# Attention scores with keys on partitions, their maximum and sum by GpSimd; reciprocals and the convolution's SiLU by ScalarE

## The chip, the core and the metric

The kernel runs on one core of a Trainium2 chip. The metric is the device time of one execution in microseconds. TensorE (PE in the profile) multiplies matrices into PSUM, VectorE (DVE) and ScalarE (ACT) work elementwise, GpSimd (POOL) too, and SyncE (SP) issues DMA transfers between HBM and SBUF. All run in parallel, each in its own order, and are tied by semaphores.

## What is computed

One layer: RMSNorm, one input projection, attention over a window and a short gated convolution beside it, one output projection, residual, RMSNorm. The part that the change touches:

```
def swa_sink_attention(q, k, v, sinks, rel_bias):       # 16 chunks of 64 frames, 16 heads, 2 kv heads of 64
    logits = jnp.einsum('bnqkgd,bnskd->bnkgqs', q, kb)   # a chunk's 64 queries x the 128 keys of its band
    logits = logits * (1.0 / math.sqrt(HEAD_DIM)) + band_bias(rel_bias)[None, None]
    logits = jnp.where(valid[...], logits, NEG)
    m = jnp.maximum(jnp.max(logits, axis=-1, keepdims=True), sink)
    p = jnp.exp(logits - m)
    denom = jnp.sum(p, axis=-1, keepdims=True) + jnp.exp(sink - m)
    o = jnp.einsum('bnkgqs,bnskd->bnqkgd', (p / denom), vb)
def short_gated_conv(h, c_gate, b_gate, conv_w, conv_b): # b_gate * causal_conv3(c_gate * h)
...
        mixed = jnp.concatenate([attn * jax.nn.silu(g_attn),
                                 conv * jax.nn.silu(g_conv)], axis=-1)
        x = x + jnp.einsum('bse,ed->bsd', mixed, w_out[l])
```

## The kernel before

**Products.** The two projections are cut into eight blocks (BLOCKS; GATES, QKV, four CONV blocks, OUT0, OUT1), each of 28 steps (LEN): seven partial products p of four steps q. A step multiplies two slices of K for four (QKV: five) tiles of 128x512, and each product is done in three parts with operands split into a high and a low half (product, L1996 to L2011), so a step is 24 matmuls of 512 columns. The high half of the weights is made by ScalarE (w_hi, L970), the low half by VectorE (w_lo, L1344), into a ring of three steps (w_ring); both are issued two steps ahead. The tiles of a finished product leave PSUM through ScalarE (copy_out, L1094) or VectorE (sums, L1483 to L1526), one step after they are done at the latest, since the next products want the banks. VectorE also forms the sums of weights that the seven products need (s1 to s4, L1436 to L1454, raw<-raw).

**Order.** Nothing is scheduled by a planner: each engine runs one loop over the steps n and the four quarters (tiles) of a step, and calls helpers where tables and conditions say so. An instruction that waits holds everything behind it on its engine.

**Attention** is spread over the convolution blocks as 32 units u (a chunk and a kv head, with 8 heads). unit_at(n, quarter) (L482) gives the unit and its offset o from 0 to 11; a unit takes 12 quarters, three steps. Before the change:

- o = 0, TensorE: probs_by_values(u - 1) (L2053), two matmuls of 512 columns; queries_by_keys(u) (L2029), for each of four pairs of heads one matmul with the queries as weights and 256 columns of k_cur (high and low keys side by side), so that queries lie on partitions and keys run along a row.
- o = 1, VectorE: shift_logits (L1564): two operations add the two score halves and the bias, with the sign turned, then a minimum over each row (129 numbers, the last one is the sink).
- o = 1, ScalarE: move_o_lo (L1154) for the unit before, two halves. o = 3: exp_logits (L1135), four exponentials that sum their rows too.
- o = 3, VectorE: gate_output(u - 1) (L1603). o = 4: normalise (L1586), a reciprocal of 128x4 and a product.
- o = 8, TensorE: turn_probs (L2043): v is transposed in every second unit, probs in four transposes into PSUM. o = 9, ScalarE: turn_v, turn_p, and o = 10, VectorE: turn_v_lo, turn_p_lo, split the transposed matrices into two halves.

The **convolution** of a block: conv_u, conv_taps (L1615 to L1637), tanh_conv on ScalarE (L1161) and conv_mix in three parts (L1639), with silu(g) made of tanh: g * (tanh(g/2) + 1) / 2. They stand at the end of a block and the start of the next. **GpSimd** issues transfers of x into x_park (L505) ahead of the stage and in OUT0, adds four times for the QKV block (L874 to L889), and takes powers for the norms.

## Time and profile before

| | us |
|---|---|
| median of 3 runs (1341.04 to 1341.61) | 1341.32 |
| the profiled execution | 1342.15 |
| its span in the profile | 1340.4 |
| TensorE busy | 1327.5 (99%) |
| VectorE busy | 908.1 (68%) |
| ScalarE busy | 543.5 (41%) |
| GpSimd busy | 90.3 (7%) |

The span begins with the first instruction and ends with the last. Busy time counts each engine's instructions once, where they overlap too. The views of the trace that are quoted further down are: the page (busy time and its course in 40 slices), waits (who waited for whom), groups of instructions by line, instructions in order of time, and busy time by stretch.

### The profile page before, as it was taken

The numbers are of one execution on the slowest core, as the hardware profiler recorded it, in microseconds if no ns is written. First come the engines' busy times: TensorE is split into PE (matmuls) and PEld (weight loads), VectorE is DVE, ScalarE is ACT, GpSimd is POOL, SyncE is SP. The second block draws the span as 40 slices with busy tenths as digits, with TensorE's granted clock in tenths as the row PEclk, the third lists the DMA queues.
The fourth block names the chain that finished last, engine by engine and source line by source line (L and its number), as shares of the span: only waits on it lengthen the run. The fifth ranks groups of instructions, "written<-read, shape, count | busy, mean of one in ns | idle before, by whom it ended". The sixth has DMA issues, their size and how long they took to land.

```text
span 1340.4 us, 16528 instructions
## 1 busy us (share of the span) xinstructions
PE 1327.5 (99%) x6038; PEld 1099.2 (82%) x6038; DVE 908.1 (68%) x1132; ACT 543.5 (41%) x946; POOL 90.3 (7%) x151
## 2 busy tenths in 40 slices
PE   9999999999999999999999999999999999999997
PEld 8887888888888888888888888888888888888886
DVE  6899766323577449975589745997439896665376
ACT  7856532232233433434334333334323444321444
POOL 1222220000000000000000000000001121100001
PEclk9999999999999999999999999999999999999999
DMA  9779995988797998779987799787898978899768
GB/s 368 288 271 373 389 351 150 319 310 318 290 297 241 308 301 277 230 219 317 302 287 249 235 312 305 225 261 244 295 348 296 326 259 287 298 306 360 267 260 301
DMA packets 167888, 390.01 MB, mean 291 GB/s; under 512 B 77920, under 2 KB 90240, under 8 KB 146176
## 3 DMA queue, kind: packets, MB, share of 16 engines
q1 hardware_dynamic: 148272, 322.08, 71.7%
q0 software_dynamic: 18240, 62.92, 12.8%
q10 hardware_dynamic: 1296, 3.96, 0.8%
q8 instruction: 48, 0.79, 0.2%
q14 instruction: 32, 0.26, 0.1%
HBM read 294.18 MB, written 98.93 MB: 293 GB/s over the span
## 4 chain that ended last, share of the span: by engine, by line
PE 91%; DVE 6%; issue 2%; DMA 1%; ACT 0%; POOL 0%; POOLq 0%; DVEq 0%; ACTq 0%
PE banks L2009 86%; PE banks L2038 1%; PE banks L2050 1%; DVE x_main L1357 1%; DVE w_ring L1344 1%; DMA x_park<-e 1%; PE banks L1969 1%; PE banks L2059 1%; PE banks L2060 1%; DVE raw L1454 0%; PE banks L1994 0%; DVE raw L1442 0%; DVE e L1502 0%; DVE raw L1436 0%; DVE z L1466 0%
## 5 line engine op out<-in xcount | busy, mean ns | idle before, releaser
L2009 PE MATMUL banks<-x_main,w_ring 128*128 128x512 f32 x2352 | 551.0, 391 | 1.0 <-DVE e L1505 0.5
L2009 PEld LDWEIGHTS banks<-x_main,w_ring 128*128 128x128 f32 x2352 | 438.5, 188 | 91.9 <-issue 1.4
L970 ACT ACTIVATE w_ring<-raw 128x1024 fp32r<-128x1024 f32 x223 | 235.5, 1056 | 544.4 <-PE banks L2009 537.6
L1344 DVE TENSOR_TENSOR w_ring<-raw,w_ring 128x1024 fp32r<-128x1024 f32 x223 | 272.9, 1224 | 218.3 <-ACT w_ring L970 216.7
L2009 PE MATMUL banks<-x_far,w_ring 128*128 128x512 f32 x1680 | 393.4, 391 | 0.1
L2009 PEld LDWEIGHTS banks<-x_far,w_ring 128*128 128x128 f32 x1680 | 313.0, 188 | 64.7 <-DVE e L1502 0.5
L2009 PE MATMUL banks<-w_ring,x_main 128*128 128x512 f32 (+1 forms) x1020 | 230.9, 387 | 0.3 <-DVE e L1502 0.3
L2009 PEld LDWEIGHTS banks<-w_ring,x_main 128*128 128x128 f32 x1020 | 189.9, 188 | 39.6 <-DVE e L1502 0.7
L505 POOL DMA_DIRECT2D x_park<-x_main x104 | 56.1, 539 | 1006.0 <-DVE x_main L1357 1005.9
L1001 ACT ACTIVATE x_main<-z 128x512 fp32r<-128x512 f32 x104 | 64.9, 624 | 116.6 <-issue 81.5
L1357 DVE TENSOR_TENSOR x_main<-z,x_main 128x512 fp32r<-128x512 f32 x104 | 71.3, 687 | 37.7 <-ACT x_main L1001 37.5
L2009 PE MATMUL banks<-w_ring,x_far 128*128 128x512 f32 (+1 forms) x348 | 78.2, 382 | 0.4 <-issue 0.4
L1094 ACT ACTIVATE e<-banks 128x512 f32<-128x512 f32 x96 | 56.7, 596 | 46.7 <-PE banks L2009 46.2
L2009 PEld LDWEIGHTS banks<-w_ring,x_far 128*128 128x128 f32 x348 | 63.8, 188 | 13.4 <-issue 0.8
L1141 ACT ACTIVATE probs<-logits,small 128x129 f32<-128x129 f32 x128 | 50.0, 393 | 43.8 <-DVE small L1584 43.7
L1572 DVE SCALAR_TENSOR_TENSOR logits<-banks,bias 128x512 f32<-128x512 f32 (+1 forms) x32 | 21.5, 672 | 44.2 <-PE banks L2038 44.2
L1442 DVE TENSOR_TENSOR raw<-raw 128x1024 f32<-128x1024 f32 x32 | 41.2, 1289 | 1.2
L1436 DVE TENSOR_TENSOR raw<-raw 128x1024 f32<-128x1024 f32 x32 | 41.2, 1287 | 0.0
L1448 DVE TENSOR_TENSOR raw<-raw 128x1024 f32<-128x1024 f32 x32 | 39.2, 1225 | 2.9
L1454 DVE TENSOR_TENSOR raw<-raw 128x1024 f32<-128x1024 f32 x32 | 39.1, 1220 | 0.4
L1516 DVE TENSOR_TENSOR e<-e,banks 128x512 f32<-128x512 f32 x24 | 16.4, 685 | 27.6 <-PE banks L2009 14.3
L1502 DVE TENSOR_TENSOR e<-e,banks 128x512 f32<-128x512 f32 x32 | 21.4, 684 | 19.2 <-PE banks L2009 19.1
(164 smaller groups left out, 845.3 us busy)
## 6 DMA issues: line engine op xcount, KB each, us to landing
x_far<-x_park SPq DMA_DIRECT2D x84, 1024.0 KB, 6.3
x_main<-x_park SPq DMA_DIRECT2D x84, 1024.0 KB, 6.1
raw<-in_w_blocks_dram SPq DMA_DIRECT2D x127, 512.0 KB, 5.4
x_park<-x_main POOLq DMA_DIRECT2D x104, 512.0 KB, 5.7
q_cur<-qkv_park SPq DMA_DIRECT2D x64, 128.0 KB, 4.9
z<-mix_park SPq DMA_DIRECT2D x16, 512.0 KB, 7.7
z<-in_x_dram SPq DMA_DIRECT2D x6, 1024.0 KB, 13.0
x_park<-e POOLq DMA_DIRECT2D x8, 512.0 KB, 6.4
```

Of the source, the lines that this page charges most:

```text
L505: engine.dma_start(x_park[0 if n < LEN else 1, n % LEN, :, i, :], x_main[:, k, :, :].rearrange("p a c -> p (a c)").bitcast(F32)).then_inc( ...
L970: act.activation(w_ring[:, n % NW, :, 0, :], raw[:, c, k:k + 2, :], ACT.Copy).then_inc(w_hi_ready, 1)
L1001: act.activation(x_halves(n)[i][:, 0, :], z[:, h, kt16, :], ACT.Copy, scale=scale).then_inc(x_hi_ready, 1)
L1094: act.activation(e_tile(b, to, t), banks[:, BANK[b, p, t], :], ACT.Copy).then_inc(copy_ready, 1)
L1141: op = act.activation(probs[:, j, :], logits[u % 2][:, j, :], ACT.Exp, bias=row_min[:, j:j + 1], scale=-1.0, accum_out=row_sum[:, j:j + 1])
L1344: dve.tensor_tensor(w_ring[:, n % NW, :, 1, :], raw[:, c, k:k + 2, :], w_ring[:, n % NW, :, 0, :], ALU.subtract).then_inc(w_lo_ready, 1)
L1357: dve.tensor_tensor(half[:, 1, :], z[:, h, kt16, :], half[:, 0, :], ALU.subtract).then_inc(x_lo_ready, 1)
L1436: dve.tensor_tensor(raw[:, 1, k, :], raw[:, 1, k, :], raw[:, 1, high, :], ALU.add).then_inc(s1_ready, 1)
L1442: dve.tensor_tensor(raw[:, 0, k, :], raw[:, 1, k, :], raw[:, 0, k, :], ALU.subtract).then_inc(s2_ready, 1)
L1448: dve.tensor_tensor(raw[:, 0, high, :], raw[:, 0, high, :], raw[:, 0, k, :], ALU.subtract).then_inc(s4_ready, 1)
L1454: dve.tensor_tensor(raw[:, 0, k, :], raw[:, 1, high, :], raw[:, 0, k, :], ALU.subtract).then_inc(s3_ready, 1)
L2009: op = pe.matmul(bank, left, right, start=(first and i == 0), stop=(kt == HK - 1 and i == 2), skip_group_check=goes_on)
```

## The change

**Scores.** queries_by_keys has the keys as weights and all 512 columns of queries (8 heads x 64) as moving data, in two matmuls that add up the high and the low keys; keys lie on partitions. The bias is stored by keys too (its table is reversed, and the sign is no longer turned), and the sinks are subtracted from it once (take_sinks). **Maximum and sum over keys** thus run over partitions: GpSimd's partition_all_reduce, once with max over logits (key_max, issued at o = 1) and once with add over probs (key_sum, o = 6), both over 128x512 with the result in all partitions. VectorE makes the scores at o = 1 in one operation (scale_logits), max(top, 0) - logits at o = 4 (shift_logits), ScalarE exp(-relu(top)), which is the sink's own term, and exp(-probs) at o = 5, VectorE adds the sink's term to the sum at o = 11 (add_sink). probs needs no transpose any more; it is split where it lies (split_p, o = 6; split_p_lo, o = 7), and is not normalised: the reciprocal of the sum is made by ScalarE as exp(-ln(total)) at o = 1 of the next unit (invert_total) and multiplied into the gate at o = 3 (weight_gate). v is transposed at o = 0. **Convolution:** ScalarE makes silu itself (silu_conv), and conv_mix has two parts. The tables are placed so, and the rule that put some w_lo half a step later (late_w) is gone.

TensorE, from one unit's products with v to the next one's. Before (k_cur, q_cur: keys and queries of the unit; pt_hi, pt_lo: the halves of its transposed probs):

```order
L2059 MATMUL banks<-pt_hi,v_cur 128x512
L2060 MATMUL banks<-pt_lo,v_cur 128x512
L2038 MATMUL banks<-k_cur,q_cur 128x256 x4
L2009 MATMUL banks<-x_main,w_ring 128x512 x24
L2009 MATMUL banks<-x_far_54,w_ring 128x512 x24
L2047 MATMUL banks<-ident,v_win 128x128
L2050 MATMUL banks<-ident,probs 128x128 x4
L2009 MATMUL banks<-x_far_55,w_ring 128x512 x24
L2059 MATMUL banks<-pt_hi,v_cur 128x512
L2060 MATMUL banks<-pt_lo,v_cur 128x512
```

and with the change:

```order
L2083 MATMUL banks<-pt_hi,v_cur 128x512
L2084 MATMUL banks<-pt_lo,v_cur 128x512
L2068 MATMUL banks<-q_cur,k_cur 128x512
L2069 MATMUL banks<-q_cur,k_cur 128x512
L2075 MATMUL banks<-ident,v_win 128x128
L2040 MATMUL banks<-x_main,w_ring 128x512 x24
L2040 MATMUL banks<-x_far_54,w_ring 128x512 x24
L2040 MATMUL banks<-x_far_55,w_ring 128x512 x24
L2083 MATMUL banks<-pt_hi,v_cur 128x512
L2084 MATMUL banks<-pt_lo,v_cur 128x512
```

The four narrow score matmuls are two wide ones, the four transposes of probs are gone, and the transpose of v stands ahead of the unit's products.

VectorE, one unit in the middle of a block. Before (small holds minimum, sum and reciprocal):

```order
L1572 SCALAR_TENSOR_TENSOR logits_71<-banks,bias 128x4x128
L1576 SCALAR_TENSOR_TENSOR logits_71<-banks,logits_71 128x4x128
L1584 TENSOR_REDUCE small<-logits_71 128x4
L1344 TENSOR_TENSOR w_ring<-raw,w_ring 128x2x512
L1609 TENSOR_TENSOR o_mix<-banks,o_lo 64x256 x2
L1613 TENSOR_TENSOR o_mix<-o_mix,g_cur 128x256
L1588 RECIPROCAL small<-small 128x4
L1590 TENSOR_TENSOR probs<-probs,small 128x4x128
L1344 TENSOR_TENSOR w_ring<-raw,w_ring 128x2x512 x2
L1596 TENSOR_TENSOR v_cur<-banks,v_cur 128x2x64
L1601 TENSOR_TENSOR pt_lo<-banks,pt_hi 128x512
```

and with the change (top: GpSimd's maximum, total: its sum, inv_row: ScalarE's reciprocal):

```order
L1605 SCALAR_TENSOR_TENSOR logits_71<-banks,bias 128x512
L1375 TENSOR_TENSOR w_ring<-raw,w_ring 128x2x512
L1631 TENSOR_TENSOR v_cur<-banks,v_cur 128x2x64
L1627 TENSOR_TENSOR g_cur<-g_cur,inv_row 128x256
L1644 TENSOR_TENSOR o_mix<-banks,o_lo 64x256 x2
L1648 TENSOR_TENSOR o_mix<-o_mix,g_cur 128x256
L1614 SCALAR_TENSOR_TENSOR probs<-top,logits_71 128x512
L1375 TENSOR_TENSOR w_ring<-raw,w_ring 128x2x512
L1636 TENSOR_TENSOR pt_lo<-probs,pt_hi 128x512
L1375 TENSOR_TENSOR w_ring<-raw,w_ring 128x2x512
L1621 TENSOR_TENSOR total<-total,sink_prob 128x512
```

Two passes over scores and the normalisation are gone, the shift stands behind GpSimd's maximum, the sink's sum behind GpSimd's sum, and the weighting of the gate ahead of the output.

ScalarE, from one unit's o_lo to the next one's. Before:

```order
L970 ACTIVATE w_ring<-raw 128x2x512
L1158 ACTIVATE o_lo<-banks 64x256 x2
L1141 ACTIVATE probs,small<-logits_72,small 128x129 x4
L970 ACTIVATE w_ring<-raw 128x2x512 x2
L1152 ACTIVATE pt_hi<-banks 128x512
L970 ACTIVATE w_ring<-raw 128x2x512
```

and with the change:

```order
L1193 ACTIVATE o_lo<-banks 64x256 x2
L1185 ACT_TABLE_LOAD
L1185 ACTIVATE inv_row<-total 64x256 x2
L1187 ACT_TABLE_LOAD
L1187 ACTIVATE inv_row<-inv_row 128x256
L1171 ACTIVATE v_cur<-banks 128x2x64
L991 ACTIVATE w_ring<-raw 128x2x512
L1161 ACTIVATE sink_prob<-top 128x512
L1163 ACTIVATE sink_prob<-sink_prob 128x512
L1165 ACTIVATE probs<-probs 128x512
L1178 ACTIVATE pt_hi<-probs 128x512
L991 ACTIVATE w_ring<-raw 128x2x512 x2
```

Exp and Ln each have a table load in front of them in the built program.

On GpSimd 64 instructions of 128x512 (top<-logits and total<-probs in turn) stand between the additions for QKV and the transfers of OUT0. The core of the diff (waits, counts and semaphores that only follow from it are left out):

```diff
-CONV_MIX1_AT = ((6, 1, 3), (6, 2, 1), (6, 2, 3))
+CONV_MIX1_AT = ((6, 1, 3), (6, 2, 3))
...
+            def key_max(u):
+                pool.wait_ge(logits_read, u + 1)
+                if u > 0:
+                    pool.wait_ge(shifted, u)
+                    pool.wait_ge(exp_done, 3 * u - 2)
+                pool.partition_all_reduce(top, logits[u % 2], P, bass.bass_isa.ReduceOp.max).then_inc(max_ready, 1)
+            def key_sum(u):
+                pool.wait_ge(exp_done, 3 * u + 3)
+                if u > 0:
+                    pool.wait_ge(inv_step, 3 * u - 1)
+                pool.partition_all_reduce(total, probs, P, bass.bass_isa.ReduceOp.add).then_inc(key_sum_ready, 1)
...
+                act.wait_ge(max_ready, u + 1)
...
+                act.activation(sink_prob, top, ACT.Relu).then_inc(exp_done, 1)
+                act.wait_ge(exp_done, 3 * u + 1)
+                act.activation(sink_prob, sink_prob, ACT.Exp, scale=-1.0).then_inc(exp_done, 1)
+                act.wait_ge(shifted, u + 1)
+                act.activation(probs, probs, ACT.Exp, scale=-1.0).then_inc(exp_done, 1)
...
+            def split_p(u):
+                act.wait_ge(exp_done, 3 * u + 3)
+                if u > 0:
+                    act.wait_ge(pv_done, u)
+                act.activation(pt_hi[:, :], probs, ACT.Copy).then_inc(pt_hi_ready, 1)
+            def invert_total(u):
+                act.wait_ge(weight_step, 2 * u + 1)
+                for par in range(2):
+                    rows = slice(par * HEAD, (par + 1) * HEAD)
+                    act.activation(inv_row[rows, :, :], total_by_half[rows, par, :, :], ACT.Ln).then_inc(inv_step, 1)
+                act.wait_ge(inv_step, 3 * u + 2)
+                act.activation(inv_row[:, :, :], inv_row[:, :, :], ACT.Exp, scale=-1.0).then_inc(inv_step, 1)
...
+            def silu_conv(b, h):
+                src = 1 if h else 3
+                act.wait_ge(sum_ready, sum_count(b, 5 if h else 4, 3))
+                act.activation(e[:, src, 2:4, :], e[:, src, 2:4, :], ACT.Silu).then_inc(conv_gated, 1)
...
+                dve.tensor_tensor(bias[:, :, :], bias[:, :, :], sink_row.unsqueeze(2).to_broadcast([P, HEADS, CHUNK]),
+                                  ALU.subtract).then_inc(edges_written, 1)
...
+                rows = slice(CHUNK if u < 2 else 0, P)
+                dve.scalar_tensor_tensor(out=logits[kv][rows, :], in0=logit_ps[rows, :], scalar=SCALE,
+                                         in1=bias[rows, kv * PAIRS * 2:(kv + 1) * PAIRS * 2, :].rearrange("p h s -> p (h s)"),
                                          op0=ALU.mult, op1=ALU.add).then_inc(logits_read, 1)
-                dve.wait_ge(logits_read, u * 2 + 1)
-                dve.scalar_tensor_tensor(out=logits[kv][:, :, lo:BAND], in0=logit_ps[:, :, 0, lo:],
-                                         scalar=-SCALE, in1=logits[kv][:, :, lo:BAND],
-                                         op0=ALU.mult, op1=ALU.add).then_inc(logits_read, 1)
-                dve.wait_ge(logits_read, u * 2 + 2)
-                if u < 2:
-                    dve.wait_ge(edges_written, 3 * KVH)
+            def shift_logits(u):
+                dve.wait_ge(max_ready, u + 1)
                 if u > 0:
-                    dve.wait_ge(exp_done, u)
-                dve.tensor_reduce(row_min, logits[kv][:, :, :], AX_X, ALU.min).then_inc(min_ready, 1)
-            def normalise(u):
-                dve.wait_ge(exp_done, u + 1)
-                dve.reciprocal(row_inv, row_sum).then_inc(inv_ready, 1)
-                dve.wait_ge(inv_ready, u + 1)
-                dve.tensor_tensor(probs[:, :, 0:BAND], probs[:, :, 0:BAND],
-                                  row_inv.unsqueeze(2).to_broadcast([P, PAIRS, BAND]), ALU.mult
-                                  ).then_inc(probs_ready, 1)
+                    dve.wait_ge(key_sum_ready, u)
+                    dve.wait_ge(pt_lo_ready, u)
+                dve.scalar_tensor_tensor(out=probs, in0=top, scalar=0.0, in1=logits[u % 2], op0=ALU.max, op1=ALU.subtract
+                                         ).then_inc(shifted, 1)
+            def add_sink(u):
+                dve.wait_ge(key_sum_ready, u + 1)
+                dve.wait_ge(exp_done, 3 * u + 2)
+                dve.tensor_tensor(total, total, sink_prob, ALU.add).then_inc(weight_step, 1)
+            def weight_gate(u):
+                dve.wait_ge(inv_step, 3 * u + 3)
+                dve.wait_ge(g_loaded, u * 16 + 16)
+                dve.tensor_tensor(g_cur[:, :, :], g_cur[:, :, :], inv_row[:, :, :], ALU.mult).then_inc(weight_step, 1)
...
-                    dve.wait_ge(conv_tanh, 2 * (b - CONV0) + (1 if h else 2))
-                    dve.scalar_tensor_tensor(out=gate, in0=at_tanh, scalar=1.0, in1=gate, op0=ALU.add, op1=ALU.mult
-                                             ).then_inc(conv_step, 1)
...
+                            scale_logits(u)
+                        elif o == 3 and u % 2 == 0:
+                            turn_v_lo(u // 2)
+                        elif o == 4:
                             shift_logits(u)
-                        elif o == 4:
-                            normalise(u)
-                        elif o == 10:
-                            if u % 2 == 0:
-                                turn_v_lo(u // 2)
-                            turn_p_lo(u)
+                        elif o == 7:
+                            split_p_lo(u)
+                        elif o == 11:
+                            add_sink(u)
                     if o == 3 and 0 < u <= UNITS:
+                        weight_gate(u - 1)
                         gate_output(u - 1)
-                    late_w = CONV0 <= b < OUT0 and i in (0, 6) and unit_at(n, 2)[1] == 10 and unit_at(n, 2)[0] < UNITS
-                    if quarter == 2 and late_w:
-                        w_lo(n + 2)
                     if quarter == 1:
-                        if W_TABLED <= n + 2 < STEPS and not late_w:
+                        if W_TABLED <= n + 2 < STEPS:
...
-                for j in range(PAIRS):
-                    op = pe.matmul(logit_ps[:, j, :, :].rearrange("p c k -> p (c k)"),
-                                   q_cur[:, 2 * j:2 * j + 2, :].rearrange("p h s -> p (h s)"),
-                                   k_cur[:, :, :].rearrange("p c k -> p (c k)"), start=True, stop=True)
...
-                    op = pe.transpose(pt_ps[:, j * P:(j + 1) * P], probs[:, j, 0:BAND], ident[:, :])
...
+                queries = q_cur[:, :, :].rearrange("p h s -> p (h s)")
+                pe.matmul(logit_ps, k_cur[:, 0, :], queries, start=True, stop=False)
+                pe.matmul(logit_ps, k_cur[:, 1, :], queries, start=False, stop=True).then_inc(qk_done, 1)
```

## Rows read from the trace of the kernel before

**Rows 1.** The page: busy time, and 40 slices of the span in tenths.

```profile
PE 1327.5 (99%) x6038; PEld 1099.2 (82%) x6038; DVE 908.1 (68%) x1132; ACT 543.5 (41%) x946; POOL 90.3 (7%) x151
...
DVE  6899766323577449975589745997439896665376
```

**Rows 2.** Waits of TensorE in the whole span: engine, line, released by, total, times, longest (us).

```profile
PE banks L1994 <- POOL ident L848: 1.5, 1, 1.5
```

**Rows 3.** Busy time by stretch: length, PE, PEld, DVE, ACT, POOL, clock, DMA, GB/s.

```profile
384.00:437.52 53.52, 53.52 (x247) 44.45 (x246) 42.27 (x61) 22.69 (x50) 0.00 (x0) 1.00 0.86 253
508.88:598.08 89.20, 89.13 (x413) 73.63 (x412) 82.23 (x111) 34.06 (x78) 0.00 (x0) 1.00 0.80 246
669.44:776.48 107.04, 107.04 (x497) 88.89 (x496) 92.30 (x124) 42.40 (x96) 0.00 (x0) 1.00 0.83 257
830.00:937.04 107.04, 106.94 (x495) 88.50 (x495) 91.17 (x122) 41.09 (x95) 0.00 (x0) 1.00 0.81 254
...
sum 214.08, PE 214.08 PEld 177.72 DVE 110.19 ACT 87.19 POOL 0.00; mean PE 53.52 PEld 44.43 DVE 27.55 ACT 21.80 POOL 0.00
```

**Rows 4.** TensorE in order of time: start, duration (us), line, out<-in, count.

```profile
412.27 11.09 PE L2009 MATMUL banks<-x_far,w_ring 128*128 128x512 f32 x48
423.19 0.60 PE L2050 MATMUL banks<-ident,probs 128*128 128x128 f32 x4
423.55 5.74 PE L2009 MATMUL banks<-x_main,w_ring 128*128 128x512 f32 x24
429.12 0.40 PE L2059 MATMUL banks<-pt_hi,v_cur 128*128 128x512 f32 x1
...
430.07 5.64 PE L2009 MATMUL banks<-x_main,w_ring 128*128 128x512 f32 x24
...
447.97 11.09 PE L2009 MATMUL banks<-x_main,w_ring 128*128 128x512 f32 x48
```

**Rows 5.** Groups of VectorE, 384 to 955 us: count, busy us, mean ns, idle before.

```profile
L1590 DVE TENSOR_TENSOR probs<-probs,small 128x512 f32<-128x512 f32 x32 | 22.2, 693 | 1.1
L1584 DVE TENSOR_REDUCE small<-logits 128x4 f32<-128x516 f32 x32 | 22.1, 691 | 1.1
L1576 DVE SCALAR_TENSOR_TENSOR logits<-banks,logits 128x512 f32<-128x512 f32 (+1 forms) x32 | 21.6, 675 | 1.1
...
L1613 DVE TENSOR_TENSOR o_mix<-o_mix,g_cur 128x256 f32<-128x256 f32 x31 | 13.2, 425 | 1.1
...
L1653 DVE TENSOR_TENSOR e<-e 128x1024 f32<-128x1024 f32 x6 | 7.3, 1222 | 0.1
...
L1588 DVE RECIPROCAL small<-small 128x4 f32<-128x4 f32 x32 | 5.5, 171 | 5.4 <-ACT probs L1141 5.4
```

**Rows 6.** Groups of GpSimd in the whole span, the same columns.

```profile
L860 POOL TENSOR_TENSOR small<-small 128x1 f32<-128x1 f32 x4 | 2.7, 681 | 0.3
L879 POOL TENSOR_TENSOR x_raw<-x_raw 128x1024 f32<-128x1024 f32 x1 | 2.4, 2405 | 25.5 <-DVE xw L1532 25.5
...
L907 POOL TENSOR_TENSOR small<-small 128x4 f32<-128x4 f32 x1 | 1.0, 1037 | 0.1
```

**Rows 7.** VectorE and GpSimd in order of time at two places of block QKV.

```profile
167.22 2.90 POOL L874 TENSOR_TENSOR x_raw<-x_raw 128x1024 f32<-128x1024 f32 x1
167.78 3.43 DVE L1436 TENSOR_TENSOR raw<-raw 128x1024 f32<-128x1024 f32 x1
...
197.40 1.72 DVE L1344 TENSOR_TENSOR w_ring<-raw,w_ring 128x1024 fp32r<-128x1024 f32 x1 [1.85 <-ACT w_ring L970]
...
198.18 3.19 POOL L884 TENSOR_TENSOR x_raw<-x_raw 128x1024 f32<-128x1024 f32 x1
```

**Rows 8.** Groups of ScalarE, 384 to 955 us, and the last row from 0 to 384 us.

```profile
L1141 ACT ACTIVATE probs<-logits,small 128x129 f32<-128x129 f32 x128 | 50.0, 393 | 43.8 <-DVE small L1584 43.7
...
L1141 ACT ACT_TABLE_LOAD x1 | 1.3, 1283 | 0.0
...
L1001 ACT ACTIVATE x_main<-z 128x512 fp32r<-128x512 f32 x48 | 29.9, 624 | 34.5 <-PE banks L2009 19.0 <-issue 12.8 <-DVE z L1369 2.7
```

More of the change, by code:

```diff
@@ L31 @@
 REL = 192
-LB = BAND + 1
 N = 512
@@ L312, in build @@
         zeros = sb("zeros", [P, CHUNK], X + 18 * KB + 1600)
-        bias = sb("bias", [P, HEADS // 2, BAND], Z)
-        logits = [sb(f"logits{i}", [P, PAIRS, LB], Z + 4096 + 2080 * i) for i in range(KVH)]
-        probs = sb("probs", [P, PAIRS, LB], Z + 8256)
-        v_win = sb("v_win", [P, BAND], Z + 10336)
-        g_cur = sb("g_cur", [P, PAIRS, CHUNK], Z + 11360)
-        o_mix = sb("o_mix", [P, PAIRS, CHUNK], Z + 12384)
-        o_lo = sb("o_lo", [P, PAIRS, CHUNK], Z + 13408)
-        q_cur = sb("q_cur", [P, PAIRS * 2, CHUNK], Z + 14432, F32R)
-        k_cur = sb("k_cur", [P, 2, BAND], Z + 16480, F32R)
-        pt_hi = sb("pt_hi", [P, N], Z + 17504, F32R)
-        pt_lo = sb("pt_lo", [P, N], Z + 19552, F32R)
-        v_cur = sb("v_cur", [P, KVH, 2, HEAD], Z + 21600, F32R)
+        bias = sb("bias", [P, HEADS, CHUNK], Z)
+        logits = [sb(f"logits{i}", [P, N], Z + 4096 + 2048 * i) for i in range(KVH)]
+        probs = sb("probs", [P, N], Z + 8192)
+        top = sb("top", [P, N], Z + 10240)
+        sink_prob = sb("sink_prob", [P, N], Z + 12288)
+        total = sb("total", [P, N], Z + 14336)
+        inv_row = sb("inv_row", [P, PAIRS, CHUNK], Z + 16384)
+        v_win = sb("v_win", [P, BAND], Z + 17408)
+        g_cur = sb("g_cur", [P, PAIRS, CHUNK], Z + 17920)
+        o_mix = sb("o_mix", [P, PAIRS, CHUNK], Z + 18944)
+        o_lo = sb("o_lo", [P, PAIRS, CHUNK], Z + 19968)
+        q_cur = sb("q_cur", [P, PAIRS * 2, CHUNK], Z + 20992, F32R)
+        k_cur = sb("k_cur", [P, 2, BAND], Z + 23040, F32R)
+        pt_hi = sb("pt_hi", [P, N], Z + 24064, F32R)
+        pt_lo = sb("pt_lo", [P, N], Z + 26112, F32R)
+        v_cur = sb("v_cur", [P, KVH, 2, HEAD], Z + 28160, F32R)
         u_buf = sb("u_buf", [P, 2, 2 + S], Z + 32 * KB - 32)
@@ L487, in conv_count @@
         def conv_count(b, i):
-            return 20 * (b - CONV0) + i
+            return 18 * (b - CONV0) + i
         def w_count(n):
@@ L1567, in shift_logits @@
                 if u == 0:
-                    dve.wait_ge(bias_loaded, 32)
-                lo = CHUNK if u < 2 else 0
+                    take_sinks()
+                    dve.wait_ge(edges_written, KVH + 2)
                 if u > 1:
-                    dve.wait_ge(exp_done, u - 1)
-                dve.scalar_tensor_tensor(out=logits[kv][:, :, lo:BAND], in0=logit_ps[:, :, 1, lo:],
-                                         scalar=-SCALE, in1=bias[:, kv * PAIRS:(kv + 1) * PAIRS, lo:],
+                    dve.wait_ge(max_ready, u - 1)
@@ L1841, in _ @@
                         if b > CONV0 and (i, q, quarter) in CONV_MIX0_AT:
-                            for part in ((0,), (1, 2))[q]:
-                                conv_mix(b - 1, 0, part)
+                            conv_mix(b - 1, 0, q)
                         if b < OUT0:
```

131 lines of the change are left out of this document (57 added, 74 removed).

## The prediction

> **What bounds the kernel now.** I read the page first, then who waits for whom on TensorE, then the attention stage in order of time. TensorE is busy for 1327.5 us of a span of 1340.4 [rows 1], at the full clock (1.00 in every stretch, [rows 3]), and its longest wait is one of 1.5 us at the start [rows 2]. Time therefore comes out only if TensorE is given less to do, and goes in wherever another engine makes it wait. The second thing to see is VectorE: 68% on average, but in the digits of its slices runs of 9 stand between runs of 3 to 5 [rows 1]. I cut the stage of the 32 attention units (384 to 955 us) there: 3, 5, 6 and 6 units lie in four bursts (384 to 437.5, 508.9 to 598.1, 669.4 to 776.5, 830 to 937), in which VectorE is busy 307.97 of 356.8 us, and twelve units in the light stretches between, with 110.19 of 214.1 (last row of [rows 3]). GpSimd does nothing in the whole stage [rows 3]. That is what the change relies on, and the bursts are where it can go wrong.
>
> **TensorE's part.** One unit is the time between two identical starts: 412.27 to 430.07 without a transpose of v, 430.07 to 447.97 with one [rows 4], so 17.85 us on average. 48 products of 512 columns, two steps, take 10.92 (412.27 to 423.19), so one matmul 0.2275 and a unit's three steps 16.38; attention takes 1.47. Its parts are the two products with v and the four 256-column score matmuls, 0.95 (429.12 to 430.07), the four transposes of probs, 0.36 (423.19 to 423.55), 0.11 more in the step behind them (423.55 to 429.12 is 5.57, not 5.46), and the transpose of v, 0.10 in every other unit, so 0.05. After the change there are two products with v and two score matmuls, all of 512 columns: 4 x 0.2275 = 0.91, with v's 0.05 and, behind it in half of the units, half of the 0.11: 1.02. **Saved: 0.45 a unit, x 32 = 14.4 us**; the new unit is 17.40 us. This lies wholly on the path. It is the most that the change can give.
>
> **VectorE's own work.** Removed in each unit: the second half of the scores 0.675, the minimum 0.691, the reciprocal 0.171, the normalisation 0.693 = 2.23. Added: shift and sink sum (both 128x512, 0.69 as the normalisation) and the weighting of the gate (128x256, 0.425 as the product in o_mix) = 1.80. Net -0.44 a unit, all by [rows 5]. The convolution loses two 128x1024 operations a block, 2 x 1.22 (e<-e, [rows 5]), which fall into bursts 2, 3 and 4. The bursts' 307.97 become 307.97 - 20 x 0.44 - 3 x 2.44 = 291.9; the light units' 110.19 become 104.9.
>
> **GpSimd's part, the unknown term.** Two reductions over 128 partitions of 512 columns a unit, 64 in all; the trace has none. I call the time of one T. Low end: a GpSimd addition of 1024 columns takes 2.40 us undisturbed [rows 6], so one pass over 512 columns is 1.2 us. High end: its power of one column takes 0.68 and of four 1.04 [rows 6], 0.12 us a further column, which over 512 gives 62 us. A reduction over partitions has to bring 128 values together, combine them and write the result into all 128, more than an addition and nothing like a power; I take three passes, **T = 3.6 us** as an estimate, far nearer to the low row. The range carries both sides.
>
> **Why T is not hidden.** The rows that decide are two places where GpSimd adds while VectorE works [rows 7]. VectorE's addition of 128x1024 takes 1.22 us; the one that starts at 167.78 beside GpSimd's of 167.22 lasts 3.43 us, to 171.21, which is GpSimd's end at 170.12 plus 1.09. It holds the other way round too: GpSimd's addition of 198.18 lasts 3.19 instead of 2.40, since VectorE's of 197.40 was still running until 199.12. So an operation of VectorE with two inputs in SBUF and a reading one of GpSimd take turns. Nearly all that fills the bursts is of that form (w_ring<-raw,w_ring; raw<-raw; y_buf<-u_buf,y_buf; e<-e), and the change makes pt_lo one as well, since it now reads probs from SBUF. 2T a unit are then added to VectorE's load although VectorE isn't the one that works. The two new waits come to the same: shift_logits stands in VectorE's queue for the maximum and add_sink for the sum, and behind them stand w_lo of the step after next and the sums of finished tiles, for which TensorE waits. On GpSimd nothing else is queued in the stage. The Trainium skill (SBUF — State Buffer, Who interferes with whom) says the same of this pair of ports; by it too, two inputs in SBUF are enough, and the trace agrees, with 3.43 us for 1.22.
>
> **The sum.** A burst of n units can take n x 17.40 us and what VectorE may fall behind before TensorE stops: a bank is wanted again one step after its tile was done, 5.46 less the 0.69 of the sum, about 5 us. Beyond it every microsecond stops TensorE. Bursts: 291.9 + 40T against 20 x 17.40 + 4 x 5 = 368.0, so 40T - 76.1; with T = 3.6 that is +67.9. Light units: 104.9 + 24T against 12 x 17.40 = 208.8, so 24T - 103.9, which is nothing below T = 4.33. Together 67.9 - 14.4 = +53.5 against the profiled execution's 1342.15 us (span 1340.4), so 1395.7; the median of the runs shown is 0.8 lower, and the forecast is **1395 us**. By the same two lines: T = 1.2 gives 1327, the break-even lies at T = 2.2 (bursts 2, 3 and 4 lose 8 + 4 + 3), T = 5 gives 1467, and from T = 4.33 on the time is 1327 + 64T - 180, so T = 7.2 gives 1608.
>
> **ScalarE.** A unit's four exponentials (4 x 0.393, and reads of their accumulators) become a relu and two exponentials of 128x512 (3 x 0.62, as the copies into x_main), and for the reciprocal two logarithms of 64x256 and an exponential of 128x256 (3 x 0.4 or a little more) [rows 8]. The built program also has two table loads a unit, one before Ln and one before Exp (the third place shown of the change; 76 rows of table loads where 3 were): 2 x 1.283 [rows 8]. Net some +3.5 on 22.69 of 53.52 us, or 7.6 a unit [rows 3], hidden by ScalarE's own idle time. The chain: the products with v done 0.46 into the unit, o_lo 2 x 0.4, then 2.57 + 1.2 for loads, Ln and Exp, so VectorE's weighting can begin 5.0 us into the unit, where its place comes at 4.1 (third quarter of a 5.46 us step). These 0.9 us fall while GpSimd holds the maximum: nothing. If GpSimd were short they would stand alone, up to 0.9 in each of twenty full units. Behind that wait stand gate_output and the next w_lo; TensorE wants that w_lo a step and a half later. The other edits (bias by another pattern, sinks in it once, edges, silu for tanh) touch transfers or instructions issued once or eight times; nothing on the path.
>
> **Rivals.**
> - GpSimd is short: T at 1.2 to 2 us. Then each burst's 291.9 + 40T stays inside what it may lose, and the 14.4 us come out: **1327** (1335 at T = 2). For: one pass is only 1.2 us. Against: the result has to cross partitions and come back. It decides at T = 2.2, and is the case on the other side of my forecast.
> - The two engines don't take turns, since this operation may hold the read port only while it reads. Then only the chain counts: scores 0.67, T, relu and two exponentials 1.9, T, sink sum 0.69, against 17.40: hidden up to T = 7. **1327** again. Against it stand the four rows of [rows 7].
> - GpSimd is slow, T = 6 to 20: 1327 + 64T - 180, so **1530 to 2430**. For: at six passes (one to fold, four halvings, one to spread) T would be 7.2.
> - T near the high end. By the row of the power, 62 us: 1327 + 64 x 62 - 180 = **5115 us**. The Trainium skill (GPSIMD Engine Reference, Cross-partition — where GPSIMD wins) gives 247.7 us for a reduction over partitions of 2048 columns; a quarter of it is the same 62, an estimate from that page. No row here shows such an operation.
> - The change saves nothing on TensorE, because two wide matmuls and the queries as moving data cost what four narrow ones and the transposes did. The starts in [rows 4] leave no room for it.
>
> **How the numbers follow.** Forecast, T between 2.3 and 6: 0.40. Short T: 0.13. No turns: 0.13. T of 6 to 20: 0.22. T near 60: 0.07. Within the bound of equal times, T around 2.2: 0.05. A measurement here can tell about 0.2%, 2.7 us. Faster 0.26, same 0.05, slower 0.69. The range goes from the full saving with some microseconds more, 1323, to T = 9, 1327 + 576 - 180 = 1723; beyond it lie about half of the slow case and the 62 us, some 0.19.
>
> **What would show it.** The new profile has 64 GpSimd operations of 128x512 whose spacing gives T; units of 17.40 us in the light stretches; operations of VectorE (raw<-raw, w_ring<-raw) that last T longer where they stand beside GpSimd; TensorE waiting for w_ring or e in the four bursts and, above T = 4.33, everywhere; a busy time of VectorE that rises though its work falls. I am wrong on the mechanism if VectorE's 1.22 us stay 1.22 beside GpSimd, and on the size alone if they stretch by another T.

## The result, and the profile after

The changed kernel takes **1329.99 us** (median of 4 runs, 1329.01 to 1330.47), the kernel before 1341.46 in the same session (1341.04 to 1341.77). The ratio is 0.9913, with a 95% interval of 0.9901 to 0.9925: **faster by 11.5 us, 0.87%**. The forecast was 1395 us, slower. The profiled execution took 1330.21 us, its span is 1328.3, and TensorE's mean granted clock is 0.999 (2.4 GHz), as before.

From the page of the changed kernel, busy time and VectorE's 40 slices, which answer to [rows 1]:

```profile
PE 1311.7 (99%) x5846; PEld 1082.0 (81%) x5846; DVE 943.9 (71%) x1089; ACT 681.3 (51%) x955; POOL 295.2 (22%) x215
...
DVE  6899766324479569995699956899548896665376
```

TensorE has 192 instructions and 15.8 us of busy time less. VectorE is busy 35.8 us *more* (908.1 before), although by [rows 5] its own work fell by 24: 32 x 0.44 and 4 x 2.44. So some 60 us of its busy time are waits inside instructions. That sign is the one the prediction named; the time came out the other way all the same.

The four bursts of the changed kernel by stretch (columns as in [rows 3]), and all waits of TensorE between 384 and 1000 us (columns as in [rows 2]):

```profile
384.00:437.50 53.50, 53.01 (x235) 43.48 (x234) 45.69 (x51) 28.51 (x42) 14.99 (x5) 1.00 0.82 251
508.90:598.10 89.20, 89.07 (x394) 73.35 (x393) 87.50 (x100) 57.34 (x82) 33.82 (x11) 1.00 0.79 246
669.40:776.50 107.10, 105.59 (x466) 86.62 (x465) 98.04 (x112) 68.61 (x98) 38.31 (x12) 1.00 0.79 257
830.00:937.00 107.00, 105.06 (x463) 85.80 (x462) 96.81 (x112) 67.35 (x98) 42.03 (x12) 1.00 0.76 250
```

```profile
PE banks L2083 <- DVE pt_lo L1636: 1.8, 3, 0.9
PE banks L2040 <- DVE e L1533: 1.2, 1, 1.2
PE banks L2040 <- ACT e L1115: 1.0, 2, 0.5
```

VectorE fills its bursts further (85 to 98% of them), but TensorE stops for only 4 us in the stage. Its unit, start to start (compare [rows 4]):

```profile
410.87 0.39 PE L2083 MATMUL banks<-pt_hi,v_cur 128*128 128x512 f32 x1
411.10 0.39 PE L2084 MATMUL banks<-pt_lo,v_cur 128*128 128x512 f32 x1
411.32 0.39 PE L2068 MATMUL banks<-q_cur,k_cur 128*128 128x512 f32 x1
411.55 0.39 PE L2069 MATMUL banks<-q_cur,k_cur 128*128 128x512 f32 x1
411.78 11.04 PE L2040 MATMUL banks<-x_far,w_ring 128*128 128x512 f32 x48
422.66 5.60 PE L2040 MATMUL banks<-x_main,w_ring 128*128 128x512 f32 x24
428.10 0.39 PE L2083 MATMUL banks<-pt_hi,v_cur 128*128 128x512 f32 x1
```

428.10 - 410.87 = 17.23 us without a transpose of v; with one it is 17.36 where nothing stalls. The mean is 17.30, against 17.85 before and 17.40 forecast.

The reductions, over the whole span, and one place where each meets VectorE (start, duration):

```profile
L912 POOL PARTITION_ALL_REDUCE total<-probs x32 | 116.7, 3646 | 155.3 <-ACT probs L1165 155.3
L906 POOL PARTITION_ALL_REDUCE top<-logits x32 | 87.9, 2748 | 365.6 <-DVE logits L1605 365.6
```

```profile
538.00 2.68 POOL L906 PARTITION_ALL_REDUCE top<-logits  x1 [7.92 <-DVE logits L1605]
544.14 3.47 POOL L912 PARTITION_ALL_REDUCE total<-probs  x1 [3.46 <-ACT probs L1165]
```

```profile
537.83 1.22 DVE L1375 TENSOR_TENSOR w_ring<-raw,w_ring 128x1024 fp32r<-128x1024 f32 x1
538.96 2.06 DVE L1467 TENSOR_TENSOR raw<-raw 128x1024 f32<-128x1024 f32 x1
...
544.56 3.15 DVE L1473 TENSOR_TENSOR raw<-raw 128x1024 f32<-128x1024 f32 x1
```

In the kernel they last 2.75 and 3.65 us, 3.2 on average; the guess of T was 3.6. So T was nearly what was forecast, and the bursts' sum 40 x 3.2 - 76.1 still says +52. What is not as forecast stands in the last fence. The maximum lasts from 538.00 to 540.68, and the operation with two inputs beside it has ended by 541.02: it is 0.84 us longer than its 1.22, not 2.7. The sum, 544.14 to 547.61, makes its neighbour 1.93 us longer, not 3.5.

### The profile page after: what moved, and what is told of

Same layout as the page of the kernel before. It is cut to its first block, busy times and chain, and to the rows that moved or that the text cites. A ratio compares the mean times of both kernels' runs of the same rounds, so it can differ in the third digit from the quotient of the medians.

```text
span 1328.3 us, 16340 instructions
## 1 busy us (share of the span) xinstructions
PE 1311.7 (99%) x5846; PEld 1082.0 (81%) x5846; DVE 943.9 (71%) x1089; ACT 681.3 (51%) x955; POOL 295.2 (22%) x215
## 4 chain that ended last, share of the span: by engine, by line
PE 75%; DVE 15%; issue 6%; ACT 2%; POOL 1%; DMA 1%; DVEq 0%; POOLq 0%; ACTq 0%
PE banks L2040 72%; DVE w_ring L1375 3%; DVE raw L1473 2%; DVE x_main L1388 1%; DVE raw L1467 1%; DMA x_park<-e 1%; POOL total L912 1%; PE banks L2000 1%; DVE pt_lo L1636 1%; DVE logits L1605 1%; DVE o_mix L1644 0%; DVE probs L1614 0%; DVE raw L1485 0%; DVE total L1621 0%; DVE e L1681 0%
## 5 line engine op out<-in xcount | busy, mean ns | idle before, releaser
L906 POOL PARTITION_ALL_REDUCE top<-logits x32 | 87.9, 2748 | 365.6 <-DVE logits L1605 365.6
L912 POOL PARTITION_ALL_REDUCE total<-probs x32 | 116.7, 3646 | 155.3 <-ACT probs L1165 155.3
L1473 DVE TENSOR_TENSOR raw<-raw 128x1024 f32<-128x1024 f32 x32 | 52.6, 1642 | 1.2
L1636 DVE TENSOR_TENSOR pt_lo<-probs,pt_hi 128x512 fp32r<-128x512 f32 x32 | 44.6, 1395 | 11.3 <-ACT pt_hi L1178 11.3
L1467 DVE TENSOR_TENSOR raw<-raw 128x1024 f32<-128x1024 f32 x32 | 50.7, 1585 | 0.0
L1485 DVE TENSOR_TENSOR raw<-raw 128x1024 f32<-128x1024 f32 x32 | 46.8, 1461 | 0.5
```

What stands on the lines that cost most here:

```text
L906: pool.partition_all_reduce(top, logits[u % 2], P, bass.bass_isa.ReduceOp.max).then_inc(max_ready, 1)
L912: pool.partition_all_reduce(total, probs, P, bass.bass_isa.ReduceOp.add).then_inc(key_sum_ready, 1)
L1467: dve.tensor_tensor(raw[:, 1, k, :], raw[:, 1, k, :], raw[:, 1, high, :], ALU.add).then_inc(s1_ready, 1)
L1473: dve.tensor_tensor(raw[:, 0, k, :], raw[:, 1, k, :], raw[:, 0, k, :], ALU.subtract).then_inc(s2_ready, 1)
L1636: dve.tensor_tensor(pt_lo[:, :], probs, pt_hi[:, :], ALU.subtract).then_inc(pt_lo_ready, 1)
```

## Experiments

Two theories stand at the start. **A**: VectorE is kept from the read port that it shares with GpSimd ("the port" below) for only a part of a reduction. **B**: for all of it, as the prediction had it, and something else gave the time back.

**The reductions alone.** A kernel of its own, with streams on both engines, started together:

> This kernel computes nothing of the reference (it copies x to the output) and times GpSimd's reductions by themselves: first alone, 128 x 256, 512, 512 and 1024 columns, maximum and then sum, and then one reduction of 512 columns beside a stream of VectorE operations that start with it: six with two SBUF operands of 1024 columns, six with one operand, six with one operand in PSUM and one in SBUF. Theory A (the port is held for only a part of a reduction, and VectorE's operations that stand back to back go first): alone 2.7 us for the maximum and 3.5 us for the sum at 512 columns; beside two-operand operations the first of them that comes after the reduction has begun is stretched by about 0.8 us (maximum) or 2.0 us (sum), less than the reduction's length; where VectorE's stream has begun first, its six operations keep their 1.22 us and the reduction is the one that is stretched, to over 8 us. One-operand operations are not stretched. Theory B (the whole length is taken in turns): a two-operand operation beside a reduction ends no earlier than the reduction's whole length plus its own 1.22 us, and each of the two waits once.

GpSimd's line of it, in order of time; a group of eight stands for the solo ones, of which two are cut out behind it (the maximum and the sum of 512 columns):

```profile
9.63 22.86 POOL L69 PARTITION_ALL_REDUCE pout<-pin  x8 [9.20 <-DVE bank L77]
...
12.65 1.78 POOL L69 PARTITION_ALL_REDUCE pout<-pin  x1
...
19.73 3.23 POOL L69 PARTITION_ALL_REDUCE pout<-pin  x1
```

Alone the maximum takes 1.06, 1.78 and 3.22 us for 256, 512 and 1024 columns, the sum 1.79, 3.23 and 6.11: the length goes with the columns, and T for this kernel's pair is 2.5. The 2.7 and 3.5 us of the kernel contain waiting. Beside VectorE (two inputs behind a one-input lead; one input; one input in PSUM):

```profile
32.66 2.31 POOL L69 PARTITION_ALL_REDUCE pout<-pin  x1 [0.17 <-POOL pout L69]
...
33.24 2.06 DVE L86 TENSOR_TENSOR result<-left,right 128x1024 f32<-128x1024 f32 x1
...
41.62 3.27 DVE L86 TENSOR_TENSOR result<-left,right 128x1024 f32<-128x1024 f32 x1
...
73.76 2.73 DVE L88 TENSOR_SCALAR result<-left 128x1024 f32<-128x1024 f32 x1
...
80.75 0.68 DVE L90 TENSOR_TENSOR result<-bank,right 128x512 f32<-128x512 f32 x1
```

Exactly one operation pays: 2.06 - 1.22 = **0.84 us beside a maximum of 1.78**, 3.27 - 1.22 = **2.05 us beside a sum of 3.23**; the five behind it keep their 1.22. The pair holds VectorE for 2.9 us a unit, 1.45 for each reduction, where the prediction charged 3.6. That is theory A. Two expectations failed. One-input operations *do* wait (2.73 for 0.68, and the one behind it takes 1.29). And a running row doesn't keep GpSimd out: in each case of this kernel the port changes hands at the end of the current operation (the long sum below is a case where it doesn't). Operations with one operand in PSUM keep their 0.68 us.

**The same, without the reductions, with twice as many, and in the kernel before.**

```diff
-pool.partition_all_reduce(top, logits[u % 2], P, ReduceOp.max)
+pool.memset(top if u == 0 else small[:, 108:109], 300.0)      # and 1.0 for total
```

> The changed kernel without its 64 reductions: maximum and total are constants written once, and in each reduction's place GpSimd writes one column of four bytes, so that what is computed of the attention is wrong and all else stays. TensorE's work stays at 17.3 us a unit. Theory A (the reductions cost VectorE 2.7 us of port a unit, nearly all of it under cover): 1323 to 1328 us, since TensorE lost some 5 to 6 us of the stage to waits and only a part of these goes. Theory B (the reductions cost VectorE their whole 6.2 us a unit, and something else gave back what the prediction had missed): 1280 to 1310 us is what would be left without them. VectorE's busy time falls by some 50 to 60 us under both.

**1324.72 us** (1323.71 to 1325.79), ratio to before 0.9878 (0.9863 to 0.9892), inside A's range. TensorE's waits for VectorE in the stage are gone. Page of this kernel, and TensorE's only waits from 384 to 1000 us:

```profile
PE 1309.1 (99%) x5846; PEld 1081.4 (82%) x5846; DVE 883.5 (67%) x1089; ACT 681.3 (52%) x955; POOL 96.3 (7%) x215
```

```profile
PE banks L2040 <- ACT e L1115: 0.9, 2, 0.5
```

So the 64 reductions cost **5.3 us**, where the prediction had 67.9, and stretch VectorE by 943.9 - 883.5 = 60.4 us, 1.9 a unit: two thirds of the 2.9 that it would be if an operation always stood ready to pay. B's 1280 to 1310 is out.

```diff
+port_in = sb("port_in", [P, N], Z + 24 * KB)       # kernel before
+pool.partition_all_reduce(port_out, port_in, P, ReduceOp.max)
+pool.partition_all_reduce(port_out, port_in, P, ReduceOp.add)
```

> The kernel before, unchanged in what it computes, with the two reductions of 128 x 512 added to each of its 32 units, on tiles of their own, at the places at which the changed kernel has them, and with nobody waiting for them. It pays the port and nothing else. The room of the four bursts in the kernel before is 48.8 us. Theory A (1.37 us of port for each of 40 half-turns, 55 us in all): +6 us, between 1341 and 1352. Theory B (3.1 us each): 40 x 3.1 - 48.8, +75 us, about 1417.

**1355.89 us** (1355.75 to 1356.88), ratio 1.0112 (1.0096 to 1.0127): +14.6, somewhat above A's range and far from B's 1417. VectorE's busy time rose from 908.1 to 970.4, 62.3 us, the same stretch as in the changed kernel. The contention alone can thus make a kernel slower. TensorE waited 10.9 us in the stage, half of it for this:

```profile
PE banks L2069 <- DVE probs L1609: 5.4, 7, 1.3
```

These are the transposes of probs, which want VectorE's product in the middle of a unit and which the changed kernel no longer has. That, and 24 us less work on VectorE, are the likely reasons that the changed kernel pays less; no run separates the two.

```diff
+pool.partition_all_reduce(dump, logits[u % 2], P, ReduceOp.max)
 pool.partition_all_reduce(top, logits[u % 2], P, ReduceOp.max)     # the sum likewise
```

> The changed kernel with each reduction done twice, the first time into a tile that nobody reads. It adds 6.2 us of GpSimd to each unit of 17.4. By the prediction's own sum (one burst unit in 40 half-turns, 76.1 us of room): theory A (2.7 us of port a unit, so 5.5 us with both) gives 40 x 2.74 - 76.1 - 14.4 above 1341, that is 1360 us, between 1335 and 1375. Theory B (12.4 us a unit on VectorE) gives 172 + 45 - 14 above 1341, about 1540 us.

**1378.07 us** (1376.83 to 1378.86), ratio 1.0272 (1.0255 to 1.0289), 3 us above A's range, and 160 below B. But this edit also makes the unit's chain longer, and TensorE now waited for its end, pt_lo. So the same load was put where nobody waits for it:

```diff
 pool.partition_all_reduce(top, logits[u % 2], P, ReduceOp.max).then_inc(max_ready, 1)
+pool.wait_ge(max_ready, u + 1)
+pool.partition_all_reduce(dump, bias[:, 0:HEADS // 2, :], P, ReduceOp.max)   # the sum likewise
```

> The changed kernel with a second maximum and a second sum in each unit, as in the kernel that did each twice, but behind the first, whose result is signalled before: nobody waits for the added ones, which read the bias (a tile that doesn't change). That kernel took 48 us more than the changed one, with 58.6 us more of busy time on VectorE and waits of TensorE for pt_lo, the end of the unit's chain. Theory P (port: the 48 us are VectorE's bursts running over): nearly all of it is here too, 1365 to 1380 us. Theory L (length: the unit's chain from the scores to pt_lo has become 5 us longer, and the port is the smaller part): VectorE is busy 58 us more again, but the time is 1340 to 1360 us.

**1373.98 us** (1370.62 to 1374.25), ratio 1.0235 (1.022 to 1.0251): 44 of the 48 us are there although none of the 64 reductions that somebody waits for had to wait for GpSimd. It is the port, through VectorE's load. The next lines show what TensorE waited for most in the stage of this kernel, then the 8.4 us around its longest stop (4.6 us, to 728.0; columns as in [rows 3]), in which VectorE is busy all the time, and one place in order of time:

```profile
PE banks L2089 <- DVE pt_lo L1642: 24.7, 11, 4.6
```

```profile
720.00:728.40 8.40, 3.77 (x17) 2.80 (x17) 8.40 (x5) 3.17 (x4) 7.68 (x2) 1.00 1.01 309
```

```profile
702.85 3.69 POOL L918 PARTITION_ALL_REDUCE dump<-bias  x1
703.37 3.26 DVE L1691 TENSOR_TENSOR e<-e 128x1024 f32<-128x1024 f32 x1
```

VectorE's operation of 1.22 us takes 3.26, for a result that nobody reads. The first pair of reductions cost 5 us and the second 44: the room in the bursts is real, and the first pair uses it up.

Not all of the 44 is waiting. TensorE's stops in the stage rose from 4 to 33 us, and its busy time from 1311.7 to 1325.5, for the same instructions. The granted clock, 1.00 in the whole stage of the changed kernel, fell to 0.50 (1.2 GHz) in six short stretches here, each of which began within 1.5 us after a stop of 1.9 to 4.6 us. One of them, with what lies before and behind it:

```profile
428.00:431.40 3.40, 1.09 (x6) 0.87 (x6) 3.40 (x4) 0.69 (x1) 1.56 (x1) 1.00 0.52 219
431.40:434.80 3.40, 3.40 (x10) 2.72 (x9) 3.37 (x6) 0.44 (x1) 0.00 (x0) 0.50 0.34 60
434.80:438.20 3.40, 3.40 (x16) 2.79 (x16) 1.70 (x2) 3.29 (x7) 2.68 (x1) 1.00 1.00 410
```

The matmuls start 0.43 us apart in it and 0.23 outside. Over the six stretches that makes some 10 us, an estimate from these spacings. The kernel with each reduction done twice had the same, some 14 us.

**Is that room really gone?** Two edits give VectorE plain work of its own.

```diff
-act.activation(conv.., ACT.Silu), two parts of conv_mix     # changed kernel
+tanh_conv as before, three parts of conv_mix
```

> The changed kernel with the convolution's gate as it was before: tanh and three operations of VectorE for each half, instead of SiLU and two. VectorE gets 2.44 us back in each of four blocks, of which two lie in the bursts. Theory A (VectorE is not the bound after the change): 1330 to 1333. Theory B (VectorE's bursts are full and each us counts): 1335 to 1340.

**1336.33 us** (1335.21 to 1336.98), ratio 0.9962 (0.9949 to 0.9975): VectorE is busy 8.8 us longer, and the time is 6.3 longer. Three of the four blocks' additions lie in the bursts, not two (from 516.9, 680.9 and 845.7 us). Some 70% of what VectorE gets is paid, so taking the convolution's edit back costs 6 of the 11.5 us gained, and theory A, that VectorE is not the bound after the change, was wrong.

```diff
-Ln, Ln, Exp by ScalarE
+dve.reciprocal(inv_row[rows, :, :], total_by_half[rows, par, :, :])     # two a unit
```

> The changed kernel with the reciprocal on VectorE: two operations of 64 x 256 into inv_row ahead of the multiplication, no logarithm, no exponential and no table loads for it (ScalarE loses 3.8 us a unit, 2.6 of it table loads). VectorE gains two short operations. Theory A (ScalarE's chain costs a few us by its queueing, VectorE has room): 1325 to 1331 us. A rival: the reciprocal is as slow on VectorE as an iterative operation may be, 0.5 us or more each, and the bursts fill up: 1331 to 1340.

**1388.12 us** (1386.61 to 1390.24), ratio 1.0351 (1.0338 to 1.0365). The group of VectorE in that kernel says why:

```profile
L1628 DVE RECIPROCAL inv_row<-total 64x256 f32<-64x256 f32 x64 | 111.5, 1742 | 1.0
```

6.8 ns a column, where the multiplication of 256 columns takes 0.43 us in all. VectorE got 3.48 us a unit, 111.5 in all, and the time rose by 58; some 14 of these are again stretches at 1.2 GHz, by the same estimate. The kernel before could afford it, with four columns ([rows 5], 0.171 us); with keys on partitions the reciprocal is of 2 x 256 columns, and with it on VectorE the change would be 46 us slower than the kernel before.

**ScalarE.** The copy of v ahead of the reciprocal:

```diff
+if o == 1 and 0 <= u < UNITS and u % 2 == 0: turn_v(u // 2)
 if o == 1 and 0 < u <= UNITS: invert_total(u - 1)
```

> The changed kernel with ScalarE's copy of the turned v (v_cur, once in two units) ahead of the reciprocal of the unit before (two table loads, a logarithm and an exponential, some 4.3 us) instead of behind it. In the changed kernel VectorE waited up to 5.7 us for that copy, 24 us in all, and TensorE idled 0.49 us at 436.60 for an eviction of ScalarE that stood behind the reciprocal. Theory A: of the 5 to 6 us that TensorE loses in the stage, this queueing on ScalarE makes up 1 to 4 us: 1326 to 1329. Theory C (TensorE's idle times come from the port alone): same, 1330.

**1329.86 us** (1329.36 to 1330.62), ratio 0.9916 (0.9902 to 0.993): no difference. VectorE's waits for v_cur are nearly gone (1.6 us), but it waits for inv_row instead, 46.6 us where it was 26.0:

```profile
DVE g_cur L1628 <- ACT inv_row L1187: 46.6, 15, 3.6
```

So this edit only changes places in ScalarE's queue, and doesn't tell what the queueing costs. With the reciprocal on VectorE as well:

> Both of the two before: the copy of v first, and the reciprocal on VectorE. Theory A: 1324 to 1329, no better than the copy of v alone by more than 2 us, since what remains is the port's. If the two are independent, their gains add.

**1388.35 us** (from 1387.31), the same as with the reciprocal alone; 1324 to 1329 was expected on the belief that the reciprocal is short. Then the table loads:

```diff
-ACT.Ln, ACT.Ln, ACT.Exp for inv_row
+ACT.Copy, ACT.Copy, ACT.Copy
```

> The changed kernel with ScalarE's reciprocal made of three copies in place of two logarithms and an exponential, so that the gate is weighted with a wrong number, and the two table loads a unit (1.283 us each, 82 us of the span) are gone while the instructions and their waits stay. The prediction costed this chain at nothing. Theory A: 1329 to 1331 us. Rival (the head of ScalarE's queue is what costs the last 5 us): 1325 to 1328 us.

**1326.87 us** (1326.7 to 1327.36), ratio 0.9891 (0.9876 to 0.9905), 3.1 below the changed kernel. The two intervals overlap a little (0.9901 to 0.9925 for the changed kernel), so this is at the edge of what can be told: the table loads of the chain that I costed at nothing cost some 3 us. VectorE's waits for inv_row and v_cur, 384 to 1000 us, first of the changed kernel:

```profile
DVE g_cur L1627 <- ACT inv_row L1187: 26.0, 8, 3.5
...
DVE v_cur L1631 <- ACT v_cur L1171: 24.3, 7, 5.7
```

and of the one without the loads:

```profile
DVE v_cur L1631 <- ACT v_cur L1171: 7.3, 6, 3.1
...
DVE g_cur L1627 <- ACT inv_row L1187: 5.4, 8, 0.9
```

**TensorE's term.**

```diff
+for j in range(PAIRS):
+    pe.transpose(v_ps[:, P:2 * P], ident[:, :], ident[:, :])
```

> The changed kernel with four 128 x 128 transposes of float32 a unit given back to TensorE (of the identity, into a free part of the bank of v, that nobody reads), as many as the change took away. It tests the term of 14.4 us. Theory A (TensorE is what bounds the stage, and its saved work is worth its full length): 1341 to 1348 us, about 11 to 18 above the changed kernel. Rival (the gain came from VectorE's lighter load, TensorE would have waited anyway): 1330 to 1336 us.

**1340.57 us** (1340.14 to 1341.58), ratio 0.9993 (0.9983 to 1.0003): +10.6 us. TensorE's busy time rose by 12.3 (1324.0 on the page), 0.38 a unit, so most of it is on the path, and the change without its saved transposes would be no gain at all. The time is 0.4 us below theory A's range; the rival, that VectorE's lighter load made the gain, had 1330 to 1336 and is out. This 10.6 and the convolution's 6.3 are each what it costs to take one edit back in the finished kernel; they are not shares of one sum.

**The long sum.** One sum of the changed kernel, at 839.80, lasted 8.81 us. It began while VectorE worked without a gap; VectorE's operations kept their 1.22 us until 845.51, and VectorE then waited 3.13 us for the sum at 848.64:

```profile
839.80 8.81 POOL L912 PARTITION_ALL_REDUCE total<-probs  x1 [5.81 <-ACT probs L1165]
```

> This kernel computes nothing of the reference (it copies x to the output). One sum of 128 x 512 by GpSimd is released after the first, second, third or fourth operation of a row of VectorE operations of the sizes that stood beside the sum of 8.81 us at 839.80 in the changed kernel (two of 512 columns, 1024, 512, 1024, 1024, 1024, all with two SBUF operands), then after the first and the third of eight of 1024 columns; then six memsets of 128 x 128 and six additions of one column by GpSimd alone and beside four operations. Theory S (a row without a gap can keep GpSimd off the port): at least one of the six sums takes 6 us or more and ends some 2 to 3 us after the row. Rival (the port is handed over at the end of the running operation, as in the first of these kernels, and the 8.81 us have another cause): all six take 3.2 to 4.5 us.

The six sums took 3.49, 4.03, 3.50, 4.03, 4.03 and 4.04 us. In each case the operation next in VectorE's row paid its 2.05, and the rest nothing. Theory S is out for the rows of this kernel. Memsets beside the same row took no more than alone and didn't stretch it; additions of one column were let in one at a time, 1.2 us apart. What made the sum of 8.81 us long stays **open**. It is no accident: in all eight variants of the changed kernel shown here that keep its reductions, the same unit's sum is long, 8.80 to 8.81 us, and 9.94 in the one with tanh, whose row is one operation longer. Each time VectorE's operations keep their lengths and the sum ends 3.1 us after the last of them, nearly its own length alone. The kernel with tanh also has a maximum of 5.29 us:

```profile
843.44 9.94 POOL L912 PARTITION_ALL_REDUCE total<-probs  x1 [5.81 <-ACT probs L1165]
```

So a row of VectorE's can keep a reduction waiting, as theory S says, but seldom, and no run shows which row: the rows of the kernel above had the sizes, not the operations themselves (the two at their head, y_buf<-u_buf,cols,y_buf, take a factor for each partition from SBUF). In the changed kernel it cost VectorE 3 us once.

## Why the prediction was wrong

- **The step that failed is the price of a reduction to VectorE: "2T a unit are then added to VectorE's load".** It put the whole length of an operation on the port. The row behind it, 3.43 us for 1.22 beside a GpSimd addition [rows 7], was read rightly, but is that of an addition, which kept VectorE waiting for 2.21 us, nearly the 2.40 that it takes undisturbed. A reduction keeps VectorE waiting for 0.84 of its 1.78 us and for 2.05 of its 3.23. With 1.45 in the place of 3.6 the same line gives 40 x 1.45 - 76.1, below zero, and **1327 us**, against 1330.0 measured. The second rival, held at 0.13, came nearest: its reason, that the operation may hold the port for only a part of its time, is what the runs show, but it said that the engines don't take turns, and they do, for 60 us of VectorE's busy time. The signs named for being wrong left this case out: VectorE's 1.22 us didn't stay, and didn't stretch by a T either.
- **The size of T** was off too: 2.5 us alone, not 3.6. By itself this wouldn't have turned the sign: 40 x 2.5 - 76.1 = +24, so 1351, above the break-even of 2.2. Only the held part lies below it.
- **The break-even was sound, its edge too sharp.** The line with 2.9 a reduction gives +40, so 1367, for the kernel with a second pair behind the first; measured were 1374. With the reciprocal's 1.74 added it gives 40 x 3.19 - 76.1 = +51.5, so 1378; measured 1388. For the kernel before with reductions it gives 307.97 + 40 x 1.45 against 20 x 17.84 + 20, nothing; measured +14.6. It is low each time, by 3 to 15 us. For the two kernels at 1374 and 1388 the stretches at 1.2 GHz (some 10 and 14 us) are as large as what is missing, and the line has no term for them. For the kernel before with reductions they aren't there: it waited for the transposes of probs, which the line doesn't have either. It may also be that the 5 us which a burst was allowed to fall behind can't be had in full. Without that allowance the kernel before gets +9, and the one with the second pair 1387, too high. No run settles how much of it is real.
- **TensorE's part** held: 14.4 us forecast; 32 x 0.55 = 17.6 by the unit, 16.5 by the kernel without reductions. The term was 2 to 3 us small: 0.05 a unit in the three steps (72 x 0.2267 = 16.33 for 16.38) and 0.05 in the attention's part (17.30 - 16.33 = 0.97 for 1.02).
- **VectorE's own savings** (24 us) held, and are worth something even now: some 70% of the convolution's part shows in the time.
- **ScalarE at nothing**: some 3 us. The mechanism written there, that the wait for inv_row stands alone if GpSimd is short, fits the kernel without table loads; its price was called up to 0.9 us in each of twenty units, and the waits were 8, of up to 3.5 us, 26.0 in all.
- **The signs named beforehand**: stretched operations (seen, 2.06 and 3.15), a busy time that rises though work falls (seen, +35.8), and TensorE waiting in the bursts for w_ring or e (hardly any: 4 us of stops in the stage, none for w_ring). The first two would have confirmed the wrong time; only the third told. The path of the wait was off too: where the bursts did run over, TensorE stood for pt_lo, the last link of the unit's chain (24.7 of 33 us in the kernel with a second pair), which the prediction doesn't name.

The account then closes to about 1 us: 1341.5 - 17.6 = 1323.9; 1324.7 measured without reductions; +5.3 for them; 1330.0.

## What to carry to other kernels

How long another engine's operation lasts is not what it costs its neighbour: find the row in which a neighbour's operation got longer, and if there is none for this kind of operation, give "held in part" as much chance as "held throughout". If the forecast hangs on a break-even, as here at 2.2 us, weigh the chances by how the terms' bounds lie about it, and not by the likeliest value. And a cost that is hidden today has used up the cover: the first pair of reductions cost 5 us, the second 44, of which some 10 because TensorE, once it had stood, was granted half the clock for a while.

## What the hardware showed that I hadn't expected

- A GpSimd reduction over 128 partitions of float32 goes by the columns: 1.78 us (maximum) and 3.23 us (sum) for 512, 3.22 and 6.11 for 1024. The row of the power, 62 us, was no guide.
- VectorE waits 0.84 and 2.05 us beside them, once (but for the long sum above), whether its operation has two inputs in SBUF or one; with one of two inputs in PSUM it doesn't wait. The one-input operation that follows runs at 1.29 instead of 0.68 us while the reduction is still under way. The rule that I had quoted from the Trainium skill (SBUF — State Buffer, Who interferes with whom), that an operation with two SBUF inputs contends with a GpSimd one that reads, is borne out. The page also says, of VectorE's two-port modes, that the loser is blocked for the whole instruction; beside a reduction the trace disagrees: the one-input operation, at 0.68 us for 1024 columns, lost 2.05 us to a sum of 3.23 and ended before it.
- VectorE's reciprocal takes 6.8 ns a column, 1.74 us for 256.
- ScalarE loads a table before each change between logarithm and exponential, 1.283 us each, 64 times in the 32 units, in the built program.
